# Half-width delta-rule inversion, and two norms applied at the drain, in a single-core chain of a four-layer and a two-layer block

## Time and profile before

| | |
|---|---|
| median of three runs | 1736.66 us (1736.13 to 1749.96) |
| the profiled execution's own time | 1722.62 us |
| its span from first to last instruction | 1720.8 us |
| mean granted TensorE clock | 0.966 of full speed |
| busy: PE, PEld | 1603.2 us (93%), 1514.6 us (88%) |
| busy: DVE, ACT, POOL | 796.1 us (46%), 808.1 us (47%), 1188.0 us (69%) |
| read from memory | 245.6 MB, 143 GB/s over the span |

### The profile page before, as it was taken

How to read it: one execution, slowest core, us unless ns; L and a number is a source line. 1 busy time by engine, 2 the same in 40 slices (tenths; PEclk the granted TensorE clock), 3 DMA queues, 4 the chain that set the end, 5 groups by cost and what they waited for, 6 DMA issues and landing times.

```text
span 1720.8 us, 32818 instructions
## 1 busy us (share of the span) xinstructions
PE 1603.2 (93%) x12776; PEld 1514.6 (88%) x12776; DVE 796.1 (46%) x1430; ACT 808.1 (47%) x1169; POOL 1188.0 (69%) x920
## 2 busy tenths in 40 slices
PE   4979999999999987999999996989999999899997
PEld 3976998999988785999999995978999999799997
DVE  6038366320166465636532004655655335575523
ACT  3473544554455435444455442555555443644442
POOL 3733994899967600098589993653899988279995
PEclk7998999999999998999999998999999999999999
DMA  5421553565544300055355552432566654155552
GB/s 213 160 88 63 172 181 111 172 196 192 191 157 154 116 1 1 13 173 181 110 173 191 193 195 72 136 111 84 175 196 195 193 168 143 58 169 193 195 196 98
DMA packets 67086, 248.55 MB, mean 144 GB/s; under 512 B 7440, under 2 KB 7696, under 8 KB 66448
## 3 DMA queue, kind: packets, MB, share of 16 engines
q1 hardware_dynamic: 66960, 246.69, 43.8%
HBM read 245.62 MB, written 1.05 MB: 143 GB/s over the span
## 4 chain that ended last, share of the span: by engine, by line
PE 52%; DVE 7%; ACT 1%; issue 1%; DVEq 0%; ACTq 0%
PE ps_dve L361 42%; PE ps_act L361 10%; DVE x_lo L1378 1%; DVE x_hi L1375 1%; PE ps_act L372 1%; DVE xT L1370 1%; DVE work L1711 1%; ACT work L977 1%; DVE work L1409 0%; DVE sq L1363 0%; DVE work L1705 0%; ACT work L931 0%; DVE sq L1343 0%; DVE xT L1328 0%; DVE x_lo L1335 0%
## 5 line engine op out<-in xcount | busy, mean ns | idle before, releaser
L326 POOL TENSOR_TENSOR ring_lo<-ring,ring_hi 128x512 fp32r<-128x512 f32 x916 | 1187.8, 1335 | 511.5 <-ACT ring_hi L917 508.5
L917 ACT ACTIVATE ring_hi<-ring 128x1024 fp32r<-128x1024 f32 x458 | 465.8, 1052 | 193.3 <-DMA ring<-panels 190.9
L361 PE MATMUL ps_dve<-x_hi,ring_hi 128*128 128x256 f32 x1728 | 415.6, 281 | 17.6 <-DVE x_lo L1378 17.4
L361 PE MATMUL ps_dve<-x_lo,ring_hi 128*128 128x256 f32 x1728 | 412.9, 279 | 0.0
L361 PEld LDWEIGHTS ps_dve<-x_hi,ring_hi 128*128 128x128 f32 x1728 | 328.8, 190 | 23.2 <-DVE x_lo L1378 18.9
L361 PEld LDWEIGHTS ps_dve<-x_lo,ring_hi 128*128 128x128 f32 x1728 | 329.1, 190 | 0.2
L361 PE MATMUL ps_dve<-x_hi,ring_lo 128*128 128x256 f32 x1728 | 243.1, 278 | 0.0
L361 PE MATMUL ps_dve<-work_parts,ring_hi 128*128 128x256 f32 x1728 | 225.3, 276 | 0.0
L361 PEld LDWEIGHTS ps_dve<-x_hi,ring_lo 128*128 128x128 f32 x1728 | 219.1, 190 | 0.2 <-POOL ring_lo L326 0.2
L361 PEld LDWEIGHTS ps_dve<-work_parts,ring_hi 128*128 128x128 f32 x1728 | 211.8, 188 | 0.0
L1370 DVE TENSOR_TENSOR xT<-xT,ps_dve 128x512 f32<-128x512 f32 x40 | 27.5, 688 | 325.7 <-PE ps_dve L361 325.1
(11 more groups left out here) (232 smaller groups left out, 2199.0 us busy)
## 6 DMA issues: line engine op xcount, KB each, us to landing
ring<-panels SPq DMA_DIRECT2D x458, 512.0 KB, 3.4
consts<-constants SPq DMA_DIRECT2D x1, 2208.0 KB, 14.8
xT<-x_t SPq DMA_DIRECT2D x1, 1024.0 KB, 5.0
memn<-mem_t SPq DMA_DIRECT2D x1, 1024.0 KB, 18.9
out_t<-xT SPq DMA_DIRECT2D x1, 1024.0 KB, 3.9
smalls<-small_operands SPq DMA_DIRECT2D x1, 849.5 KB, 7.9
consts<-constants SPq DMA_DIRECT2D x1, 129.5 KB, 4.8
angle_i<-positions SPq DMA_DIRECT2D x1, 128.0 KB, 6.3
```

The costliest lines, as they stand in the source:

```text
L326: pool.tensor_tensor(ring_lo[:, s, cs], ring[:, s, cs], plain(ring_hi[:, s, cs]), ALU.subtract).then_inc(sem("lo_made"), 1)
L361: ins = pe.matmul(o, lhsT, rhs, start=start, stop=stop, skip_group_check=True)
L917: tell(act.activation(ring_hi[:, n % RING, :], ring[:, n % RING, :], ACT.Copy), "hi_made")
```

## The change

Three things are changed; the stream of panels stays as it is.

1. The first norm. A small transfer brings the first gains ahead of everything; DVE makes `x_hi`, `x_lo` from `xT * gain` as soon as `x` is there (`stream`); the squares are summed behind the first bank; the banks of the q, k and gate projections move from `ps_act` to `ps_dve`, and DVE multiplies each by the factor as it drains it (`scaled`). Token-major value banks are scaled by ACT with a column per token (`norm_columns`). The sines' angles are worked out later. The large constants and small operands are loaded behind the first panels.
2. The inversion. At level k only the even blocks of `t` and `y` and the odd blocks of `tt` change; matmuls take these as moving operands of 64 columns instead of 128, through views with runs of 2^k elements, and `renew` works on 256 columns. ACT copies the even half of `y` and writes zeros to the odd half. `cut` now stands ahead of `renew`. The SiLU of the gate is split over levels; the head norms of both halves and both calls of `mix_heads` move behind the inversions, beside the memory projections.
3. The double norm. The MLP's `residual` makes parts from `xT` times both gains at once; ACT makes a second set of squares with the first gain; one bank holds both sums; DVE and ACT work out one joint factor, by which banks are multiplied as they are drained. `renorm` of `xT` moves behind the ropes, ahead of the norm of the compressed keys. The forgetting attention's q and k banks go to `ps_dve` and are drained between rounds of the top-64 choice.

The core of the diff, its indentation shortened by eight:

```diff
+def even(m, k):
+    return m.rearrange("p j (a two w) -> p (j a) two w", two=2, w=1 << k)[:, :, 0, :]
+def odd(m, k):
+    return m.rearrange("p j (a two w) -> p (j a) two w", two=2, w=1 << k)[:, :, 1, :]
+def dense(o, k):
+    return o[:, 0:2 * P].rearrange("p (a w) -> p a w", w=1 << k)
...
+    early = SMALLS["xa_norm"][0]
+    sp.dma_start(smalls[:, 0:early], smalls_in[:, 0:early]).then_inc(sem("gains_here"), 16)
     sp.dma_start(xT[:, :, :], x_in).then_inc(sem("stream_here"), 16)
-    sp.dma_start(consts[:, 0:first], consts_in[:, 0:first]).then_inc(sem("smalls_here"), 16)
-    sp.dma_start(angle_i[:, :], pos_in.partition_broadcast(P)).then_inc(sem("smalls_here"), 16)
-    sp.dma_start(smalls[:, :], smalls_in).then_inc(sem("smalls_here"), 16)
+    sp.dma_start(consts[:, 0:first], consts_in[:, 0:first]).then_inc(sem("ones_here"), 16)
     for s in range(RING):
-        if s == 3:
+        if s == 2:
+            sp.dma_start(angle_i[:, :], pos_in.partition_broadcast(P)).then_inc(sem("smalls_here"), 16)
             sp.dma_start(consts[:, first:], consts_in[:, first:]).then_inc(sem("consts_here"), 16)
+        if s == 4:
+            sp.dma_start(smalls[:, early:], smalls_in[:, early:]).then_inc(sem("smalls_here"), 16)
         sp.dma_start(ring[:, s, :], panels[s]).then_inc(panel_here[s], 16)
...
+    def norm_and_gates_ab():
+        pe.wait_ge(sem("ones_here"), 16)
+        norm_sums()
+        told.more("w_if_gained")
         o = bank("dve", "gate_sums")
         w_if = small("w_if").rearrange("p (k c) -> p k c", k=C)
-        narrow(o[0:ML_H, 0:T], w_if, sq, 0, 4)
-        narrow(o[0:ML_H, T:2 * T], w_if, sq, 4, 8, who="dve")
-    project("act", "act_out", x_parts, C, 8, need=pairs_of("normed"), then=gates_ab)
+        narrow(o[0:ML_H, 0:T], w_if, xT, 0, 4)
+        narrow(o[0:ML_H, T:2 * T], w_if, xT, 4, 8, who="dve")
+    project("dve", "ab_scaled", x_parts, C, 8, need=pairs_of("stream_parts"), then=norm_and_gates_ab)
...
+                    pe.wait_ge(sem("t_ready"), t_at[g] - (k > 1))
                     o = bank("act", "y_ready")
                     for j in range(4):
-                        mm(o[:, j * P:(j + 1) * P], gd_b[:, 4 * g + j, :], gd_t[:, 4 * g + j, :], True, True,
+                        js = slice(4 * g + j, 4 * g + j + 1)
+                        mm(o[:, j * 64:(j + 1) * 64], gd_b[:, 4 * g + j, :], even(gd_t[:, js, :], k), True, True,
...
+                        mm(o[:, j * 64:(j + 1) * 64], gd_tt[:, 4 * g + j, :], even(gd_y[:, js, :], k), True,
+                           True, "dve" if j == 3 else None)
                 o = bank("dve", "t_ready")
                 for j in range(4):
-                    mm(o[:, j * P:(j + 1) * P], gd_y[:, 4 * g + j, :], gd_tt[:, 4 * g + j, :], True, True,
+                    js = slice(4 * g + j, 4 * g + j + 1)
+                    mm(o[:, j * 64:(j + 1) * 64], gd_y[:, 4 * g + j, :], odd(gd_tt[:, js, :], k), True, True,
...
+    def delta_norms(i):
+        for g in {1: (0, 1), 2: (2, 3)}.get(i, ()):
+            pe.wait_ge(sem("osq"), osq_at + 2 * g + 2)
+            mm(bank("act", "norm_used"), ones, sq[:, 2 * g:2 * g + 2, :], True, True, "act")
+    osq_at = told.seen["osq"] - GD_H
+    memory_side(delta_norms)
...
+    def norms_and_gates_even():
+        o = bank("act", "norm_used")
+        told.more("squares_added")
+        for k in range(2):
+            mm(o[:, 0:T], ones, sq[:, k, :], k == 0, k == 1)
+        for k in range(C):
+            if k % 2 == 0:
+                told.more("gained_squares")
+            mm(o[:, T:2 * T], ones, memn[:, k, :], k == 0, k == C - 1, "act" if k == C - 1 else None)
+        told.more("w_fi_gained")
...
-    project("act", "act_out", x_parts, C, 4, need=pairs_of("normed"), then=gates_even)
+    project("act", "act_out", x_parts, C, 4, need=pairs_of("stream_parts"), then=norms_and_gates_even)
     rope_from = told.seen["act_out"]
-    project("act", "act_out", x_parts, C, 2, skip=(1,))
-    ckv_at = told.seen["act_out"]
+    project("dve", "ckv_raw", x_parts, C, 2, skip=(1,))
...
+    project("dve", "fox_qk", x_parts, C, 8)
     project_tokens("act", "act_out", x_parts, 2)
+    pe.wait_ge(sem("fox_qk"), told.seen["fox_qk"])
...
+            for i in (c, c + 1) if gain is not None else ():
+                ins = act.activation(memn[:, i, :], xT[:, i, :], ACT.Square, scale=gain[:, i:i + 1])
+            if gain is not None:
+                tell(ins, "gained_squares")
...
+    reach("ab_in", 1)
     rsqrt(T, 1.0 / D)
...
+    reach("ab_in", 5)
+    told.more("angles")
+    act.activation(sinT[:, :], angle[:, 0, :], ACT.Sin)
+    tell(act.activation(cosT[:, :], angle[:, 1, :], ACT.Sin), "tables")
+    def values_ab(dst):
+        o = pair(take())
+        for t in range(TT):
+            ins = act.activation(dst[:, t, :], o[:, t, :], ACT.Copy, scale=norm_col[:, t:t + 1])
+        tell(ins, "act_out")
+    reach("ab_in", 7)
+    told.more("norm_columns", TT)
...
-        if half == 0:
-            settle()
-            tell(act.activation(gate, gate, ACT.Silu), "gate_silu")
-            log_exp()
         for k in range(1, LEVELS):
             for g in range(2):
-                copy_out(gd_y[:, 4 * g:4 * g + 4, :], name="y_ready")
+                y = gd_y[:, 4 * g:4 * g + 4, :]
+                act.activation(even(y, k), dense(take(), k), ACT.Copy)
+                tell(act.activation(odd(y, k), dense(const("ones"), k), ACT.Copy, scale=0.0), "y_ready")
+            if half == 0 and k <= 4:
+                gs = gate[:, 2 * k - 2:2 * k, :]
+                tell(act.activation(gs, gs, ACT.Silu), "gate_silu")
+        log_exp()
...
+    memory_side(1, 0, 2)
+    for g in range(4):
+        if g == 2:
+            memory_side(1, 2, 3)
+        if g >= 2:
+            told.more("mixed")
+        rsqrt(2 * T, 1.0 / P)
+    memory_side(1, 3, 4)
...
+    reach("even_in", 1)
+    copy_out(ev[:, 0:2, :])
+    log_exp()
+    o = take()
+    both = rstd[:, state["norm"] % 2, :]
+    state["norm"] += 1
+    told.more("norms_joined")
+    act.activation(both[:, 0:T], o[:, 0:T], ACT.Ln, bias=eps, scale=1.0 / D)
+    step(act.activation(both[:, T:2 * T], o[:, T:2 * T], ACT.Ln, scale=1.0 / D))
+    tell(act.activation(both, both, ACT.Exp, scale=-0.5), "rstd")
...
+    def stream(c, gain):
+        for i in (c, c + 1):
+            ins = dve.tensor_scalar(x_hi[:, i, :], xT[:, i, :], gain[:, i:i + 1], None, ALU.mult)
+        step(ins)
+        for i in (c, c + 1):
+            ins = dve.scalar_tensor_tensor(x_lo[:, i, :], xT[:, i, :], gain[:, i:i + 1],
+                                           plain(x_hi[:, i, :]), ALU.mult, ALU.subtract)
+        tell(ins, "stream_parts")
...
+    dve.wait_ge(sem("gains_here"), 16)
+    dve.wait_ge(sem("stream_here"), 16)
+    for c in range(0, C, 2):
+        stream(c, small("mix_norm")[:, 0:C])
+    gained("w_if", 8, small("mix_norm")[:, 0:C])
+    first = take()
+    F = factors(T, keep=stream_f[:, :])
+    f = spread(F, 2)
+    def scaled(dst, o, scale=1.0):
+        tell(dve.scalar_tensor_tensor(dst, pair(o), scale, f, ALU.mult, ALU.mult), "ab_scaled")
+    scaled(sb_q[:, 0:2, :], first, P ** -0.5)
+    o = take()
+    r = lambda i: ab_rows[0:ML_H, i, :]
+    dve.tensor_tensor(r(3), o[0:ML_H, 0:T], F[0:ML_H, :], ALU.mult)
+    step(dve.tensor_tensor(r(4), o[0:ML_H, T:2 * T], F[0:ML_H, :], ALU.mult))
+    dve.tensor_scalar(r(3), r(3), small("ab_b_i", ML_H), None, ALU.add)
+    tell(dve.tensor_scalar(r(4), r(4), small("ab_b_f", ML_H), None, ALU.add), "gate_sums")
+    dve.wait_ge(sem("ones_here"), 16)
+    dve.wait_ge(sem("smalls_here"), 32)
...
-            if half and s == 2:
-                told.more("gate_silu")
-                mix_heads(0)
...
+        def renew(m, k):
+            tell(dve.tensor_tensor(m, m, dense(take(), k), ALU.subtract), "t_ready")
...
+                told.more("y_ready")
                 if k < LEVELS - 1:
-                    renew(gd_t, g)
                     cut(k + 1, g)
-                renew(gd_tt, g)
+                    renew(even(gd_t[:, 4 * g:4 * g + 4, :], k), k)
+                renew(odd(gd_tt[:, 4 * g:4 * g + 4, :], k), k)
...
+    told.more("gate_silu", 4)
+    mix_heads(0)
     mix_heads(1)
...
+    mlp(1, both_gain[:, :])
+    n = norm_banks[state["norm"]]
+    F, both = stream_f[:, :], rstd[:, state["norm"] % 2, :]
+    state["norm"] += 1
+    m = ps_act[:, n % BANKS, :]
+    settle()
+    dve.wait_ge(sem("act_full"), n + 1)
+    step(dve.tensor_scalar(F, m[:, 0:T], EPS * D, None, ALU.add))
+    tell(dve.scalar_tensor_tensor(m[:, T:2 * T], F, EPS, m[:, T:2 * T], ALU.mult, ALU.add), "norms_joined")
+    told.more("rstd")
+    dve.scalar_tensor_tensor(m[:, 0:T], m[:, 0:T], EPS * D, both[:, 0:T], ALU.add, ALU.mult)
+    step(dve.tensor_tensor(m[:, T:2 * T], m[:, T:2 * T], both[:, T:2 * T], ALU.mult))
+    step(dve.scalar_tensor_tensor(m, m, -0.5 / D, both, ALU.mult, ALU.mult))
```

(58 more changed lines are left out.)

166 lines of the change are left out of this document (61 added, 105 removed).

## The result

The changed kernel takes 1750.3 us, median of 20 runs (1739.63 to 1764.51), beside 1739.43 us for the kernel before on the same chips (1727.13 to 1755.96, 20 runs). The ratio is 1.0073, 95% interval 1.0046 to 1.0100: slower by 0.7%, where 1694 us was forecast. The profiled execution took 1748.08 us with a span of 1746.3. That of before took 1722.62, less than any of these 20 runs of before, so the two traces differ by 25.5 us where the medians differ by 10.9.

A forecast was written before the change was run, and what follows sets the result against it. TensorE's streaming at 0.1134 us a matmul was taken as the bound, with gains only where it does not stream. Terms of 15 + 11 + 16 = 42 us gave 1694 us, 2.4% faster, range 1672 to 1717.

The forecast's parts named there:

- term 2 (b): Inversion levels in the delta rule: 64-column records at 0.11 us, a level 5.3 us instead of 5.80; 6 us won.
- Term 1: First norm, at the start: gate columns end at 33.4 instead of 49.2 us, less a 2 us stall; 15 us won.
- Term 2 (a): Delta rule, preparation of half 1: `mix_heads(0)` and two sums of squares leave the path; 8 + 1.8 us won.
- Term 2 (c): Memory projections: added rsqrt and `mix_heads` stall TensorE 3 to 4 us, moved sums take 1.8; 5 us lost.
- Term 3: Double norm between the blocks: 17.8 instead of 39.9 us to the gate columns' end, 6 stalled behind; 16 us won.
- within 1%: Outcome class for the whole kernel: measured time less than 1%, 17 us, from before; chance 0.05.
- Slower than before: Rival, inversion levels: moving operands read through short runs make records cost four times 0.11 us; 1875 us, chance 0.03.
- over 6 the strided reads: Sign in the profile after: inversion levels of over 6 us would prove that moving reads with gaps cost more.
- By columns: Rival, inversion levels: a matmul costs by its columns, so 20 us more are won; 1674 us, chance 0.07.
- The half width brings nothing at all: Rival, inversion levels: 64 columns win none of the 6 us counted; 1700 us, inside the range, no chance of its own.

The follow-up runs named there:

- the warm start: The changed kernel with 16 extra products of 512 columns ahead of level 1 in each half of the inversion: 1718.16 us, one run.

## Why the prediction was wrong

The step that failed is in term 2 (b): "So on 128 x 128 weights a record costs some 0.11 us however few its columns; I take 0.11: 5.3 us for a level". The first half holds: narrow and wide records cost the same at either clock (16 records of level 1 at 0.50: 679.07 to 683.05 before with 128 columns, 673.59 to 677.46 after with 64; a level at 1.00: 5.57 and 5.52). The second half took for granted that the levels run at full clock. The rows for the price, and the level in the earlier trace rows were all read at full clock, and nothing asked how TensorE gets there. The preparation ahead of the levels is waits and small matmuls, and it leaves the clock at 0.50 in both kernels (675 to 683 us before; after, it falls between 671 and 677). Before, the wide products of level 1 raise it: the first two drains of `y` in half 1 lie 7.5 us apart (681.24 and 688.76), the next 5.67 and 5.80. After, it never rises. From the first drain of `y` in the first of six levels to that in the last, the inversion takes 30.6 us before and 51.6 after, in each half, and from there to the first drain of the products behind it 2.2 more: 46.4 us lost in both halves, where 6 were to be won.

Point by point:

- **Term 1, 15 us.** 19.0 at the gates, 18.6 at the stick-breaking scores. The mechanism held, and the size came out at the upper end of the range. The first bank took 8.6 us (10.97 to 19.60) instead of the 11.9 that I kept from before: its records start 0.21 us apart until 14.3 us and 0.11 to 0.12 apart behind it. (The clock row has 1.00 from 10 us on, so it doesn't show this change.) The wait for `angles` never reached TensorE: the list of its waits is empty from 30 to 75 us, where I had put 2 us of stall.
- **Term 2 (a), 8 + 1.8 us.** From the start of half 1 to its first `y` it is 15.2 us (658.40 to 673.59) against 24.9 (654.22 to 679.07), 9.7 less, where 8 were forecast. Before, the clock there was 0.50 from 669.6 us on; after, it stayed at 1.00 up to 671. The sums of squares ahead of it, 2.1 us (652.13 to 654.22), are gone as well: 11.8 in all against 9.8, the right mechanism and a somewhat larger size.
- **Term 2 (b), +6 us.** -46.4, above. At full clock it would have been 5.80 less 5.52, 0.28 us for each of ten levels, 2.8 us: half of even the small gain that I counted was not there, since 0.115 and not 0.11 is a record's price in this stream.
- **Term 2 (c), -5 us.** The memory stage took 51.7 us (742.45 to 794.1) against 45.8, 5.8 more. Of these 1.6 are the sums of half 1, which stood just ahead of the first mark before (723.50 to 725.09): 4.2 against 5, right. The waits in it are 2.5 us, not 3 to 4.
- **Term 3, 16 us.** 39.9 us to the end of the gate columns became 18.6, against 17.8 forecast: right. The wait for the compressed keys was 7.46, against 6: right. I priced a wait as its own length alone. The clock falls during it, and the matmuls behind it pay once more, 1.8 us for each of two groups. From the last add to `w_uk` 7.8 us were won, not 16. Of the 21.3 won at the gates 13.5 were lost behind them: 7.46 in the wait, 1.8 in the cold first group, 1.75 in another wait just ahead, for the rope, which the sum has at nothing, and 2.5 spread over the weight stream and the matmuls that the wait splits. And 6.3 of the 7.8 are given back by the end of the span: 3.6 by DVE's first rope ahead of the scores of the forgetting attention (1140.48 before, 1163.33 after), the cold matmuls among them, and the rest in the attentions. With `renorm` moved the wait and the fall of the clock are gone.
- **The rivals.** The result, 0.7% slower, lies in the class "within 1%", which I gave 0.05 and only as something unforeseen. *Slower than before* had the arithmetic that fits and the wrong reason: with 0.213 us a record, 0.092 over before in 544 records, it gives 50 less 36, 14 us slower, where 10.9 were measured. It needed 0.22 and named 1875 us, and I gave it 0.03 because I could name only the gaps as a cause. Its sign, "over 6 the strided reads", would have misled: the levels came out at 10.2, and the reads were innocent. *By columns* is refuted by the levels at 5.5 us. *The half width brings nothing at all* described the kernels that enter the narrow levels at full clock, where the width is worth 0.05 us a level.

The sum of the rest held by the medians. Without the half-width levels 36 us were forecast (15 + 9.8 - 5 + 16). With the old inversion the measured gain is 36.4 us (1740.37 less 1703.98). That it fits so closely is in part luck: Term 1 gave 3.6 to 4 us more and (a) 2 more, Term 3 gave 8 less. And the two traces of the ledger show less. There the levels and the products right behind them lose 48.7 us (both halves, from level 1's start to the end of those products), so the rest wins 23 of the 36. The traced execution of before was 17 us faster than its median and that of after 2, which accounts for most of the gap.

A page bears on the failed step. The Trainium skill, TensorE: Matmul & The Clock Gate (section What's actually happening), says that "the default state is throttled, and activity releases the throttle". The runs agree that it takes work to release it, and show that the busy time in the records is not the measure of that work: 20.00 of 20.00 us busy, twice over, and the clock stays at 0.50. The same page prices a load of 128 columns at 107 ns (section LDWEIGHTS (loading the stationary operand)). That agrees with 0.115 us a record at full clock and not with 0.213 at half.

Left open: why 64 columns don't raise the clock where 128 do. The changed kernel and the one with wide products differ in that width and in what the drains read, with the same weights, counts and full busy time; they don't show what the chip looks at. It also stays open where 3.3 us went between the gates of layer 1 and the first inversion. In the cross-attention TensorE waited 6.1 us for `x_lo`, where it waited 2.0 before. The wait is 6.1 or 2.9 in the traces of the other kernels that have the new norms, and 2.3 with the half width alone. So 0.9 us may be the norms'; what makes it 6.1 in some executions is open.

## What to carry to other kernels

A price read at full clock holds only if the new stream reaches full clock by itself: for each stage look at the clock it is entered with, and at which matmuls raise it. Cutting the columns of float32 matmuls on full 128 x 128 weights from 128 to 64 won almost nothing here (5.57 and 5.52 us a level; records of 4 and 65 columns took 0.116 and 0.107 us), and it took away the very work that had raised the clock; if it must be narrow, make the first level wide. Count a TensorE wait such as those of 7.5 to 9.2 us here as longer than it is, for the clock fell in them and the matmuls behind paid too.

## What the runs showed of the hardware

- The clock has memory in this stream: identical 64-column matmuls run at 0.50 and 0.213 us a record if entered at 0.50, and at 1.00 and 0.115 if entered at 1.00. Each state lasted as long as the levels: 59 us after, 33 us with the warm start.
- The granted clock can stay at 0.50 while TensorE and its weight loads both show 20.00 of 20.00 us busy.
- Moving operands with gaps, runs of 2 to 32 elements, cost nothing: 10.24 us a level against 10.24 contiguous at 0.50, and 5.52 against 5.57 for wide contiguous ones at 1.00.
- `renorm`'s eight operations of 128 x 256, 0.47 us for the shortest such one, took 8.29 us, 1.04 each, while GpSimd was busy for most of the time, and 6.25 at the later place.
